# Modulation weights from ScalarE's queue at consecutive pairs, X and Y in half as many loads, and the first expert slot's rows added in the last expert's chunk

## The reference, cut to what matters

```python
m = einsum('nd,de->ne', cond, w_ada[l]) + b_ada[l]     # 6*1024 columns, for two conditions
x = residual(x, gt1, mixer(adaln(x, norm_attn[l], sh1, sc1)))
x = residual(x, gt2, routed_moe(adaln(x, norm_ffn[l], sh2, sc2)))   # x + gt2 * (g0*y0 + g1*y1)
```

## Time and profile before

| | us |
|---|---|
| median of 3 runs | 1893.29 (1893.01 to 1895.04) |
| the profiled execution, its own time | 1897.15 |
| its span, first to last instruction | 1895.4 |
| PE busy | 1631.1 (86%) |
| VectorE busy | 1207.6 (64%) |
| ScalarE busy | 932.4 (49%) |
| GpSimd busy | 242.2 (13%) |

### The profile page before, as it was taken

The page is one execution under the profiler, slowest core; times in us unless marked ns, Lnnn a source line. Parts: engine busy times, 40 slices in busy tenths (PEclk is TensorE's granted clock), DMA queues, the critical chain, the costliest instruction groups (busy, mean ns, idle before and its releaser), DMA issues. The chain is left out here.

```text
span 1895.4 us, 32729 instructions
## 1 busy us (share of the span) xinstructions
PE 1631.1 (86%) x11909; PEld 1325.4 (70%) x11910; DVE 1207.6 (64%) x1728; ACT 932.4 (49%) x1438; POOL 242.2 (13%) x361
## 2 busy tenths in 40 slices
PE   3998886799895999999949989789979679999992
PEld 0798675687553888888838986678855468888881
DVE  1478453556346996996664883646654579899664
ACT  2254642233323886886543445323341278888651
POOL 0000035111000111111020000541200011111112
PEclk7899998999896999999969999879999889999996
DMA  8241356654305997997553110665331489999754
GB/s 339 78 151 48 100 153 163 189 178 143 137 34 205 412 405 294 380 408 269 211 218 112 56 48 1 174 197 157 95 129 53 167 304 402 408 397 409 296 198 178
DMA packets 186803, 392.96 MB, mean 207 GB/s; under 512 B 88682, under 2 KB 106114, under 8 KB 161094
## 3 DMA queue, kind: packets, MB, share of 16 engines
q1 hardware_dynamic: 163374, 326.12, 47.7%
q10 hardware_dynamic: 14824, 34.39, 4.6%
q0 software_dynamic: 8496, 30.94, 4.3%
HBM read 345.95 MB, written 45.45 MB: 207 GB/s over the span
## 5 line engine op out<-in xcount | busy, mean ns | idle before, releaser
L2363 DVE TENSOR_TENSOR expert_w_lo<-shared,expert_w_hi 128x2048 fp32r<-128x2048 f32 x192 | 433.4, 2287 | 58.3 <-ACT expert_w_hi L2302 58.3
L2302 ACT ACTIVATE expert_w_hi<-shared 128x2048 fp32r<-128x2048 f32 x192 | 366.5, 1913 | 44.1 <-PEq L146 39.6
L2229 PE MATMUL ps<-expert_w_hi,expert_x_hi 128*128 128x512 f32 x592 | 245.2, 414 | 11.0 <-DVE expert_x_lo L2358 9.2
L2231 PE MATMUL ps<-expert_w_hi,expert_x_lo 128*128 128x512 f32 x592 | 233.2, 394 | 0.0
L2230 PE MATMUL ps<-expert_w_lo,expert_x_hi 128*128 128x512 f32 x592 | 233.1, 394 | 0.0
L2229 PEld LDWEIGHTS ps<-expert_w_hi,expert_x_hi 128*128 128x128 f32 x592 | 113.5, 192 | 42.5 <-issue 12.9
L2231 PEld LDWEIGHTS ps<-expert_w_hi,expert_x_lo 128*128 128x128 f32 x592 | 112.3, 190 | 24.3
L2230 PEld LDWEIGHTS ps<-expert_w_lo,expert_x_hi 128*128 128x128 f32 x592 | 112.8, 191 | 18.7
L2284 PE MATMUL ps<-expert_w_hi,expert_hid_hi 128*128 128x512 f32 x296 | 115.8, 391 | 0.5 <-ACT expert_hid_hi L2337 0.5
L2199 POOL COPY expert_cur_idx<-slot_tokens 128x1 int32 x37 | 48.4, 1307 | 530.2 <-PE ps L2216 530.2
L2285 PE MATMUL ps<-expert_w_lo,expert_hid_hi 128*128 128x512 f32 x296 | 115.3, 390 | 0.0
(11 more groups left out here) (380 smaller groups left out, 3376.7 us busy)
## 6 DMA issues: line engine op xcount, KB each, us to landing
shared<-in_w_up SPq DMA_DIRECT2D x64, 1024.0 KB, 7.4
shared<-in_w_down SPq DMA_DIRECT2D x64, 1024.0 KB, 9.4
shared<-in_w_gate SPq DMA_DIRECT2D x64, 1024.0 KB, 8.3
qkv<-in_w_ada SPq DMA_DIRECT2D x20, 1280.0 KB, 6.1
shared<-in_w_in SPq DMA_DIRECT2D x10, 2048.0 KB, 9.2
y_table<-expert_y ACTq DMA_DIRECT2D x37, 512.0 KB, 8.5
qkvT<-in_w_ada SPq DMA_DIRECT2D x20, 768.0 KB, 8.5
setup_ada_ring<-in_w_ada SPq DMA_DIRECT2D x8, 1024.0 KB, 12.2
```

Of the source, the lines that this page charges most:

```text
L2229: pe.matmul(bank, x_hi[:, at], w_hi[:, j, w], start=(q == 0), stop=False)
L2231: return pe.matmul(bank, x_lo[:, at], w_hi[:, j, w], start=False, stop=(q == KD - 1))
L2302: act.activation(w_hi[:, j, :], raw[:, j, :], ACT.Copy).then_inc(w_hi_done, 1)
L2363: dve.tensor_tensor(w_lo[:, j, :], raw[:, j, :], w_hi[:, j, :].bitcast(F32), ALU.subtract).then_inc(w_lo_done, 1)
```

## The change

1. **Units at consecutive pairs.** `self.pairs` becomes 1, 2, 3, ... (1 to 12 in layer 0, 1 to 8 in layer 1).
2. **Their loads from ScalarE's queue.** `load_after` leaves SyncE's list; ScalarE calls it at the end of `take(n)`. Unit 0's load stays on SyncE.
3. **Half as many X and Y loads.** The tables in HBM are laid out by step, so that both directions of X (and of Y) come in one DMA for each half: 2 instead of 4. The corner blocks (`bl_load`) and QK (`qk_load`) come in 1 instead of 2.
4. **An earlier place for the first scatter.** `scatter(0)`, `x_load(0)`, `y_load(0)` stand ahead of `base_load(3)` in SyncE's list instead of behind it.
5. **Slot 0 in the last expert's chunk.** When all chunks but the last are stored and the last weights are split, GpSimd gathers the rows of slot 0 into the shared buffer: tiles 0 and 1 in layer 0 (into piece 5), all 5 tiles in layer 1. In the last chunk, VectorE waits for `gate_in` and adds tiles 0 and 1 (two operations a tile), ahead of its wait for the last product and of the `y_low` copy.
6. **What is left for later.** `Joined` gathers 8 tiles of rows instead of 10 and needs two operations for tiles 0 and 1. `combine_phase` gathers 5, has nothing on ScalarE, and VectorE first adds slot 0 of tiles 2 to 4, then slot 1 of all five, two operations each.

```diff
-        self.pairs = [1, 3, 5, 6, 8, 9, 10, 11, 13, 14, 16, 17] if l + 1 < DEPTH else [1, 3, 5, 7, 9, 11, 13, 15]
+        self.pairs = list(range(1, len(self.todo) + 1))
...
-    def load_after(self, sp, n):
+    def load_after(self, act, n):
         i = self.of_pair(n)
         if i is not None and i + 1 < len(self.todo):
-            sp.wait_ge(self.done, i + 1)
-            self.load(sp, i + 1)
+            act.wait_ge(self.done, i + 1)
+            self.load(act, i + 1)
...
                 def take(n):
                     nk = len(pair(n)[2]) * P
                     act.wait_ge(s_["pt_p"], n + 1)
                     act.activation(pT[:, :, 0:nk], G.ps[:, 6:8, 0:nk], ACT.Copy).then_inc(s_["pt_taken"], 1)
+                    units.load_after(act, n)
...
                 def x_load(s):
...
-                    for d in range(2):
-                        for b in range(2):
-                            sp.dma_start(X[half(b), d], large(A.base_x, place(s, d), b)[:, d * DH:(d + 1) * DH]).then_inc(s_["xy_in"], 16)
+                    for b in range(2):
+                        sp.dma_start(eight_of(X, b), large(entry(A.base_x, 2 * s, 2), b)).then_inc(s_["xy_in"], 16)
...
                     if i + 1 < FRONT:
                         front_out(i + 1)
+                        if i == 2:
+                            scatter(0)
+                            x_load(0)
+                            y_load(0)
                         base_load(i + 1)
-                    units.load_after(sp, i)
-                    if i == 2:
-                        scatter(0)
-                        x_load(0)
-                        y_load(0)
                     units.store_after(sp, i)
...
                 total = pool.value_load(R.base[0:1, NE:NE + 1], min_val=1, max_val=MAXC)
+                pool.wait_ge(w_lo_done, NE * PIECES)
+                pool.sem_inc(passed, 1)
+                pool.wait_ge(y_out, total * 16)
+                pool.sem_inc(passed, 1)
+                half.gathers(pool)
...
+                    if last and final:
+                        dve.wait_ge(G.gate_in, 16 * (l + 1))
+                        for t in range(EARLY):
+                            half.dve_sum(dve, t)
                     for j in range(2, 4):
                         next_lo(j)
                     dve.wait_ge(y_p, k + 2)
                     dve.wait_ge(y_out, k * 16 + 16)
                     dve.tensor_copy(y[:, 512:1024], G.ps[:, 6, :]).then_inc(y_low, 1)
...
+class FirstHalf:
...
+    def dve_sum(self, dve, t):
+        G, a = self.G, self.rows[:, t, :]
+        dve.wait_ge(self.got[t], 16)
+        dve.scalar_tensor_tensor(out=a, in0=a, scalar=self.R.gates[:, 0, t:t + 1], in1=G.gate_view[:, int(t > 0), :],
+                                 op0=ALU.mult, op1=ALU.mult).then_inc(self.scaled, 1)
+        dve.wait_ge(self.scaled, t + 1)
+        dve.tensor_tensor(G.x[:, t, :], G.x[:, t, :], a, ALU.add).then_inc(self.summed, 1)
...
                 dve.wait_ge(G.gate_in, 16 * (l + 1))
+                for t in range(EARLY, NT):
+                    first_half(t)
                 for t in range(NT):
...
+                    second_half(t)
```

More of the change, by code:

```diff
@@ L382, in gathers @@
         for t in range(NT):
-            for n in range(2):
+            for n in range(int(t < EARLY), 2):
                 pool.indirect_dma_start(out=self.place(t, n), out_offset=None, in_=self.A.y_table,
@@ L405, in dve_sum @@
         G, a, b = self.G, self.place(t, 0), self.place(t, 1)
+        g, w = G.gate_view[:, int(t > 0), :], self.R.gates[:, 1, t:t + 1]
         if t == 0:
             dve.wait_ge(G.gate_in, 16 * self.l)
[L408 to L412, removed]
+        if t < EARLY:
+            dve.wait_ge(self.got[t], 16)
+            dve.scalar_tensor_tensor(out=b, in0=b, scalar=w, in1=g, op0=ALU.mult, op1=ALU.mult).then_inc(self.gated, 1)
+        else:
+            dve.wait_ge(self.first, t - EARLY + 1)
+            dve.scalar_tensor_tensor(out=b, in0=b, scalar=w, in1=a, op0=ALU.mult, op1=ALU.add).then_inc(self.both, 1)
+            dve.wait_ge(self.both, t - EARLY + 1)
+            dve.tensor_tensor(b, b, g, ALU.mult).then_inc(self.gated, 1)
@@ L1149, in mixer_phase, with place, both, mine @@
         blocks = lambda b, c=0: G.ps[:, b, 256 * c:256 * (c + 1)].rearrange("p (h n) -> p h n", h=DH)
[L1151 to L1157, removed]
-            return of.rearrange("e (r n) -> r e n", n=HB)
+        def place(i, d):
+            g = group(i)
+            first, n = (0, 1, 3)[g], (1, 2, 2)[g]
+            return 2 * first + d * n + i - first
+        def both(table, s, size):
+            a, b = (place(ORDER.index(t), d) for d, t in enumerate(tiles(s)))
+            return table[0:2 * NT * size].rearrange("(f x) -> f x", x=size)[a:b + 1:b - a]
+        def mine(table, i, size):
+            return table[0:2 * NT * size].rearrange("(f x) -> f x", x=size)[place(i, 0):place(i, 1) + 1:place(i, 1) - place(i, 0)]
+        def entry(table, at, n=1):
+            return table[at * BASE:(at + n) * BASE]
+        def small(of):
+            of = of.rearrange("(q x) -> q x", x=SB * HB + SB)[:, 0:SB * HB]
+            return of.rearrange("q (r n) -> q r n", n=HB)[:, :, 0:SB]
+        def large(of, b):
+            of = of.rearrange("(e c x) -> e c x", c=2, x=HB * HB + HB)[:, b, 0:HB * HB]
+            return of.rearrange("e (r n) -> r e n", n=HB)
+        def step_of(i, d):
+            t = ORDER[i]
+            return NT - t if d and t else t
+        def paired(of):
+            return of.rearrange("f (p n) -> p f n", p=P)
         eight_of = lambda a, b: a[half(b)].rearrange("p d h n -> p (d h) n")
@@ L1201, in qk_load @@
                     sp.wait_ge(s_["qk_out"], 16 * (NT - 1))
-                    for d in range(2):
-                        sp.dma_start(QK[:, d].rearrange("p h n -> p (h n)"),
-                                     A.qk_table[place(s, d), :, d * DH * P:(d + 1) * DH * P]).then_inc(s_["qk_in"], 16)
+                    sp.dma_start(QK.rearrange("p d h n -> p d (h n)"), paired(both(A.qk_table, s, P * DH * P))).then_inc(s_["qk_in"], 16)
                 def scatter(i):
@@ L1223, in y_load @@
                         sp.wait_ge(s_["yf_done"], at(s - 1, 1))
-                    for d in range(2):
-                        for b in range(2):
-                            sp.dma_start(Y[half(b), d], large(A.base_y, place(s, d), b)[:, d * DH:(d + 1) * DH]).then_inc(s_["xy_in"], 16)
+                    for b in range(2):
+                        sp.dma_start(eight_of(Y, b), large(entry(A.base_y, 2 * s, 2), b)).then_inc(s_["xy_in"], 16)
                 sp.dma_start(sinks[:, :], A.sink[l:l + 1, :].to_broadcast([P, NH])).then_inc(s_["par_in"], 16)
@@ L2409, in combine_phase @@
         ph = Phase(nc, ctx, "combine", l)
-        yy = ph.sb("yy", [P, NT, 2, D])
-        gate = G.gate_view
+        yy = ph.sb("yy", [P, NT, D])
+        late = G.carve(0, (NT, D))
         got = [ph.dma_sem(G.soft[f"y_got{t}"]) for t in range(NT)]
-        first, both, gated, added, x_out = (ph.sem(n) for n in ("first", "both", "gated", "added", "x_out"))
+        scaled, summed, gated, added, x_out = (ph.sem(n) for n in ("late_scaled", "late_summed", "gated", "added", "x_out"))
         with nc.Block() as block:
@@ L2430, in _ @@
                 for t in range(NT):
-                    pool.wait_ge(got[t], 32)
-            @block.scalar
-            def _(act):
-                for t in range(NT):
-                    act.wait_ge(got[t], 32)
-                    act.activation(yy[:, t, 0, :], yy[:, t, 0, :], ACT.Copy, scale=R.gates[:, 0, t:t + 1]).then_inc(first, 1)
+                    pool.wait_ge(got[t], 16)
             @block.vector
             def _(dve):
+                gate = lambda t: G.gate_view[:, int(t > 0), :]
@@ L2496, in build @@
         G.soft = {n: top.enter_context(nc.semaphore(n)) for n in
-                  ["gathered"] + [f"y_got{t}" for t in range(NT)]}
+                  ["gathered"] + [f"y_{n}{t}" for n in ("got", "early") for t in range(NT)]}
         A.mod_rows = [nc.dram_tensor(f"mod_rows{l}", [2, 6 * D], F32, kind="Internal").ap() for l in range(layers)]
```

87 lines of the change are left out of this document (50 added, 37 removed).

## The result

| | us |
|---|---|
| before, median of 4 runs beside it | 1893.15 (1892.66 to 1895.04) |
| after, median of 4 runs | 1996.82 (1994.89 to 1997.96) |
| ratio after to before | 1.0545, 95% interval 1.0526 to 1.0563 |
| the profiled execution of after, its own time | 1994.89 |

The change costs 5.5%. The forecast was 1981 us in a range of 1940 to 2020. The page of after, against the earlier trace rows: nearly as much work of PE in a span that is 97.7 us longer.

What follows compares the result with a forecast made beforehand. Prediction: PE, busy 86% of the span and strictly in order, would stall on unit loads. 69.5 (mixer waits) + 19.5 (clock) + 5 (seam) - 6.6 (end) = 87.4 us on 1897.15, less 3.9 to the median: 1981 us, range 1940 to 2020.

Steps and rivals of the forecast that it cites:

- new stalls, 18: In both mixers, PE stalls for unit weights at 18 loads: 60.9 us in layer 0, 41.7 in layer 1, together 102.6 us.
- old waits gone: In both mixers, PE's present waits go: 19.7 us for modulation weights and 13.4 us for X and Y, together 33.1 us.
- clock, as it reaches the path: In both mixers, PE's slower clock after a stall costs 1.5 us for each of 13 stalls, 19.5 us.
- seam: Layer 0's last chunk into layer 1: late gate rows delay the y copy 7.1 us, fewer gathers return 2: costs 5 us.
- end: In `combine_phase`, VectorE need not wait for the first gathers and ScalarE, and does 16 operations, not 15: 6.6 us less.
- How long a load takes: Unit loads in the mixers: 9.0 us from first issue to landing, bounds 7.9 and 10.0, from SyncE's figures.
- When it is issued and when PE wants it: In the mixers, only the gap from the start of `take(n)` to the end of `scores(n+1)`, 1.7 to 4.2 us, hides a load.
- What it gives back: In the mixers, X and Y come while PE stands at pairs 2 to 4, so their 13.4 us of waits go.
- Short loads: Rival: unit loads in the mixers take 7.9 us each, with no clock loss: 1942 us; chance 8 in 100.
- free loads: Rival: ScalarE's unit loads in the mixers land within 4.2 us and all stalls go: 1859 us; chance 4 in 100.
- Absorbed stalls: Rival: VectorE and ScalarE catch up during PE's mixer stalls; half of 69.5 us goes, clock half as dear: 1936 us; 10 in 100.
- The one that spoke of 10 us loads: Rival: in the mixers the clock stays low between stalls and loads take 10.0 us: 2019 us; chance 8 in 100.

Runs made afterwards that it cites:

- e2: The changed kernel with the unit loads back on SyncE at their old places in its list, units still at consecutive pairs: 1934.66 us, ratio to before 1.020.
- e3: The changed kernel with ScalarE's unit loads moved from behind `take` to behind the exponentials of the pair, one block earlier: 1910.52 us, ratio to before 1.0081.
- e4: The changed kernel with the unit pairs and SyncE unit loads as before, all other parts of the change kept: 1898.22 us, ratio to before 1.0010.
- e9: The changed kernel with 60 added products, results overwritten, ahead of PE's wait for each unit's weights but a mixer's first: 1983.15 us.
- e5: The changed kernel with the gate rows' load issued ahead of layer 1's first loads in layer 0's last expert: 1991.05 us.
- e8: The changed kernel with old pairs, SyncE unit loads as before, and the gate rows' load ahead of the next layer's first loads: 1891.81 us, ratio to before 0.9982.
- e10: The changed kernel with old pairs, ScalarE's unit loads behind the exponentials, and gate rows ahead of the next layer's first loads: 1872.26 us, ratio to before 0.9886.
- e6: The changed kernel without the second DMA (0.75 MB) of each unit load behind a mixer's first: 1886.46 us, a total not comparable because tokens go to other experts.
- e1: The changed kernel with only the list of unit pairs undone, loads still on ScalarE behind `take`: 1913.58 us, ratio to before 1.0096.
- e7: The changed kernel with 120 added products, results overwritten, ahead of PE's wait for each unit's weights but a mixer's first: 1992.34 us.

## Why the prediction was right, and where its sizes were off

Against the sum, profiled execution against profiled execution: forecast +87.4 us, measured 1994.89 - 1897.15 = +97.7 us (the terms measured sum to 97.4; 0.3 us lie ahead of mixer 0). The mechanism held at each step. Sizes were off in both directions, and that the sum came so near is in part luck: the stalls were put 21.3 us too low and the clock 9.4 us too high.

| term | forecast | measured |
|---|---|---|
| new stalls, 18 | 102.6 | 123.9 |
| old waits gone | -33.1 | -33.1 |
| clock, as it reaches the path | +19.5 | +10.1, the rest of the mixers' 100.9 |
| seam | +5 | +6.2 |
| end | -6.6 | -7.3 |
| layer 1's tail and experts | 0 | -2.4 |

1. **How long a load takes** is the term that was mis-sized most. Summed over the 18 units, a unit's first product comes on average 10.33 us behind the load's first issue, where I took 9.0: 24 us more. The prediction took SyncE's figure and SyncE's bounds because no row showed this queue; with 11.9 us to land one of the loads lies outside them. The 18 are not alike: from 9.05 to 12.44 us from first issue to first product, and both layers have long ones at the same places, 12.44 and 12.13 behind pair 5, 11.04 and 11.37 behind pair 3. Beside those of pair 5, SyncE issues X and Y loads in both layers (343.11 to 346.99 us in layer 0); whether that is the cause was not tried. e2 has the same loads at consecutive pairs on SyncE, and they land in 8.1 us at the median, against 9.5 in after.
2. **When it is issued and when PE wants it.** From the first issue to the end of `scores(n+1)` it is 62.0 us over the 18 units (10.33 x 18 less 123.9), where I had 59.4. The stalls at the first pairs were 7.61, 6.78 and 8.00 us, forecast 7.3, 6.8 and 6.4; the others in layer 0 4.88 to 9.64 where I had 4.8 to 6.2. e3 shows that this place sets the loss: earlier by one block, the waits fall by 85 us.
3. **What it gives back.** Right for X and Y. (Four issues of 0.62 us against two of 0.64 are 1.2 us less, not the 1.3 of the text; no term hangs on it.) e4 shows why it is no gain of the smaller number of loads: without PE's stalls most of that wait is back.
4. **The clock.** Forecast 1.5 us for each of 13. The unit's products alone grew by 72.6 - 47.3 = 25.3 us, more than the 19.5. But PE's busy time grew by only 11.8 us in mixer 0 (193.9 to 205.7, the rows above) and 1.1 in mixer 1 (187.3 to 188.4), 12.9 us in all, because other products ran faster than before: those of a step (line 1403, now 1449) took 37.1 us in mixer 1 instead of 41.7. And PE's waits for VectorE's `norm` fell from 33.2 to 29.2 us, so part of the rest was absorbed. The sum had only a part of this: it took off 7.5 us, for half of the ten waits that go. e9 gives back some 7 to 14 us with most units at the full pace, less than the 19.5 of the sum.
5. **The seam.** As forecast: the gate rows landed 18.4 us behind their issue (forecast 16.0) and all four operations stood behind them. From that issue to the copy of y it took 23.4 us instead of 13.9, 9.5 later where I had 7.1, and the start of layer 1 gave back 3.3 where I had 2. e5 confirms the cause. That the seam would then win 2 us was wrong: VectorE waits for the gathered rows.
6. **The end.** The gathers and gate rows are in time, VectorE works 1959.35 to 1964.33 without a gap and starts again at 1969.57. Right to 1 us.
7. **The rivals.** Short loads and free loads are out: no load of the 18 was shorter than 8.6 us for its second DMA. Absorbed stalls are out: the mixers lost 100.9 us, more than the 90.8 by which the waits for weights, X and Y grew (123.9 - 33.1). The one that spoke of 10 us loads had the load about right, but not its clock, low all the way between stalls: PE's busy time would have grown by far more than 12.9 us.

Open: why loads from ScalarE's queue land later. The second DMA took 8.8 to 9.8 us at the median in the seven kernels with two-part loads from ScalarE, 8.1 to 8.5 in the four with loads from SyncE (before, e2, e4, e8). So the queue goes with the difference, but the moments differ too: the first DMA took 7.1 to 7.4 us behind `take` and 6.3 and 6.1 us behind the exponentials (e3, e10), from the same queue, where SyncE's took 6.0 to 6.2. The Trainium skill, "DMA: Bandwidth & Descriptors", section "Queues, rings and completion order", says that each DMA engine takes turns between the queues that have work for it. That would let SyncE's small transfers delay a load that in one queue would have stood ahead of them. No run here isolates it. Nor was the halving of the X and Y loads tried by itself.

## What to carry to other kernels

With one buffer, the distance that counts is from "buffer free and issued" to "engine wants it": add it up for each use ahead of moving a load, in the place in the list where the issue really stands. When an issue moves to another engine's queue, look at what stands ahead of it in that engine's list: `take` waits for PE, so a load behind it starts only just before PE wants it. Here one block earlier was worth 86 us, and with uses spread out and the gate rows first it turned a loss of 5.5% into a gain of 1.1%. When work is moved into a gap, look at what its operands are queued behind: the gate rows cost 6 us at one place in SyncE's list and nothing at another (5.8 us between after and e5, 6.4 between e4 and e8).

## What the hardware showed that was not expected

- A 2 MB load in two DMAs, issued from ScalarE while SyncE issues small ones, landed 9.5 us (8.6 to 11.9) behind its second issue; from SyncE 8.1 us (7.4 to 8.8) at the same pairs and 8.3 us (7.3 to 9.4) in e4. The two kinds were issued at different moments, so the queue alone is not shown as the cause.
- Stores of unit rows can be late when units come close together: VectorE waited for one 18.0 us in two waits in after, 17.4 us once in e3, 9.5 us once in e6, 9.3 us once in e9 and 8.1 us once in e5. It did not wait for one in the kernels with the old pairs (before, e1, e4, e8, e10), nor in e2 and e7, so consecutive pairs alone don't bring it about. In after most of it lay beside PE's own stalls (behind the one that ended at 304.11 us PE waited 1.62 us more); in e3 it cost PE 12.5 us.
- Behind 60 added products in a stall eleven of 18 units ran their first 40 products at the full clock (1.30 us), though PE still idled up to 3.88 us between the two; the four units at 2.36 us came after idle times of 2.88 to 5.06 us, those at 1.30 us after 1.83 to 3.88. The length of the last gap alone does not decide it.
